# A chunked recurrence on TensorE: token rows of every head in the other half of the partitions, and 64x64 products of channels and tokens alternated with those of a triangular inverse

## The reference, cut to what matters

```python
def step(s, inp):
    r_t, k_t, v_t, kk_t, a_t, w_t = inp
    sa = jnp.einsum("dbhij,dbhj->dbhi", s, kk_t)
    s = (s * w_t[..., None, :] - sa[..., :, None] * (kk_t * a_t)[..., None, :]
         + v_t[..., :, None] * k_t[..., None, :])
    y = jnp.einsum("dbhij,dbhj->dbhi", s, r_t) if readout else None
    return s, y
```

## Time and profile before

| | |
|---|---|
| median of 3 runs | 2006.18 us (2003.2 to 2009.24) |
| the profiled execution's own time | 2008.59 us |
| its span, first to last instruction | 2006.8 us |
| TensorE matmuls busy | 1891.1 us, 94% |
| VectorE, ScalarE, GpSimd busy | 764.0, 476.8, 243.3 us |
| the recurrence, first to last level or y product | from 1193.8 to 1448.3 us |

### The profile page before, as it was taken

One profiled execution on the slowest core, in us unless ns is written; L12 is line 12 of the kernel. 1 busy time (PEld: TensorE's weight loads), 2 busy tenths in 40 slices (PEclk: granted clock), 3 DMA queues, 4 the chain that ended last, 5 costly groups with the idle time before them and its releaser, 6 DMA issues.

```text
span 2006.8 us, 33615 instructions
## 1 busy us (share of the span) xinstructions
PE 1891.1 (94%) x13862; PEld 1003.6 (50%) x13862; DVE 764.0 (38%) x1546; ACT 476.8 (24%) x982; POOL 243.3 (12%) x295
## 2 busy tenths in 40 slices
PE   6999999999999999999899959988898999999997
PEld 2455775444444444434355438888733444444443
DVE  3551441111111100022332347766432888988001
ACT  3022552200000000033211544444322222221001
POOL 1150111000000000012000035465200000000000
PEclk9999799999999999999899979999999999999999
DMA  5421001233432223333311200000021222222222
GB/s 206 168 74 66 30 1 63 97 133 126 147 128 82 84 95 126 105 115 137 118 53 53 69 1 5 5 4 4 15 78 63 74 73 81 75 73 73 84 84 94
DMA packets 43861, 158.63 MB, mean 79 GB/s; under 512 B 5016, under 2 KB 5672, under 8 KB 42712
## 3 DMA queue, kind: packets, MB, share of 16 engines
q1 hardware_dynamic: 37440, 133.19, 19.7%
q10 hardware_dynamic: 6296, 23.58, 3.2%
HBM read 152.01 MB, written 6.31 MB: 79 GB/s over the span
## 4 chain that ended last, share of the span: by engine, by line
PE 88%; DVE 5%; ACT 5%; issue 1%; POOL 1%; DMA 0%; ACTq 0%; DVEq 0%; POOLq 0%
PE psum L330 46%; PE psum L1202 21%; PE psum L1990 2%; PE psum L1994 2%; PE psum L995 2%; PE psum L976 1%; PE psum L589 1%; PE psum L1152 1%; DVE mem L2149 1%; PE psum L963 1%; PE psum L1750 1%; PE psum L632 1%; PE psum L1342 1%; PE psum L2001 1%; DVE mem L2177 1%
## 5 line engine op out<-in xcount | busy, mean ns | idle before, releaser
L330 PE MATMUL psum<-mem 128*128 128x512 f32 (+1 forms) x2272 | 963.0, 582 | 30.3 <-DVE mem L483 15.3
L330 PEld LDWEIGHTS psum<-mem 128*128 128x128 f32 x2272 | 427.4, 190 | 536.4 <-issue 521.3
L1202 PE MATMUL psum<-mem 128*128 128x512 f32 x960 | 421.1, 598 | 4.1 <-DVE mem L2463 2.6
L1202 PEld LDWEIGHTS psum<-mem 128*128 128x128 f32 x960 | 181.7, 191 | 235.7 <-issue 228.0
L2544 DVE SCALAR_TENSOR_TENSOR mem<-mem 128x512 f32<-128x512 f32 x352 | 235.1, 746 | 0.0
L386 POOL TENSOR_TENSOR mem<-mem 128x512 f32<-128x512 f32 x24 | 30.4, 1267 | 1082.4 <-ACT mem L370 1082.0
L1990 PE MATMUL psum<-mem 64*64 64x64 f32 x1920 | 74.5, 222 | 11.7 <-DVE mem L2177 4.4
L1295 ACT ACTIVATE mem<-mem 128x512 f32<-128x512 f32 x22 | 13.9, 630 | 290.7 <-DVE mem L1311 290.7
L1231 DVE SCALAR_TENSOR_TENSOR mem<-psum,mem 128x512 f32 x16 | 12.0, 751 | 179.1 <-PE psum L1202 179.1
L1994 PE MATMUL psum<-mem 64*64 64x64 f32 x1920 | 71.2, 221 | 2.6 <-issue 2.4
L1990 PEld LDWEIGHTS psum<-mem 64*64 64x64 f32 x1920 | 65.0, 136 | 17.3 <-DVE mem L2177 10.0
(11 more groups left out here) (341 smaller groups left out, 1758.8 us busy)
## 6 DMA issues: line engine op xcount, KB each, us to landing
mem<-in_units SPq DMA_DIRECT2D x248, 512.0 KB, 3.4
mem<-in_cw ACTq DMA_DIRECT2D x2, 2048.0 KB, 10.3
mem<-in_wn ACTq DMA_DIRECT2D x1, 2048.0 KB, 8.7
bias_tiles<-bias_scratch ACTq DMA_DIRECT2D x1, 2048.0 KB
mem<-bias_tiles ACTq DMA_DIRECT2D x1, 2048.0 KB, 10.3
mem<-in_xT ACTq DMA_DIRECT2D x1, 2048.0 KB, 9.6
x_scratch<-mem ACTq DMA_DIRECT2D x1, 2048.0 KB, 8.7
mem<-x_scratch ACTq DMA_DIRECT2D x1, 2048.0 KB, 7.8
```

The lines of the kernel that those rows point to most:

```text
L330: last = pe.matmul(dst, ring[:, slot, k, :], rhs(k), start=(k == 0), stop=(k == 7))
L1202: last = eng.matmul(ps[m % 4], ring[:, slot, k - 8 * part, :], rhs(k), start=(k == 0), stop=(k == ktiles - 1))
```

## The change

`FLIP` goes: every head now has its token rows in the half opposite to its channel rows. Levels, fresh, ym and u stay in the straight quarters, and every product between channels and tokens falls into the crossed ones. In TensorE's program seven of the groups are split by direction, and each is issued within a level, one product of the level and one of the group in turn; where a group has a second function, that follows in a run of its own for each `i`. The groups move: x into level 0, raw_beta from after level 4 into level 2, y into level 3, raw_kappa into level 4, state from after level 3 into level 5, turn_v into level 7, turn_bk into level 8. PSUM is laid out anew (level products of a direction share one bank, 0 or 1; the groups have banks 2 to 7), and waits follow it. On VectorE mask_beta stays ahead of grow 5, and move goes from there to ahead of grow 9. Core of the diff:

```diff
-            FLIP = (2, 3)
             E_, O_ = [(0, 0), (1, 0)], [(0, 1), (1, 1)]
             X_ = U_ = Y_ = [(2, 0), (2, 1)]
-            YM_ = [(3, 2), (3, 3)]
-            V_ = S_ = G_ = [(3, 0), (3, 1)]
-            BETA = [(2, 0), (2, 2)]
-            KAPPA = BK = [(3, 0), (3, 2)]
+            S_ = [(2, 2), (2, 3)]
+            YM_ = [(6, 2), (6, 3)]
+            V_ = G_ = [(6, 0), (6, 1)]
+            BETA = [(4, 0), (4, 2)]
+            KAPPA = BK = [(6, 0), (6, 2)]
...
-            def tok(hp, b):
-
-                return ch(1 - b if hp in FLIP else b)
+            def tok(b):
+
+                return ch(1 - b)
...
-                def level(n, d, it):
+                def level(n, d, it, beside=(), done=None):
...
+                    a, b_ = (g[:, :, 1], T) if n % 2 == 0 else (Tt, Z) if n < 9 else (Z, Tt)
+                    at = O_[d] if n % 2 else E_[d]
+                    for i in range(2):
+                        for hp in (i, i + 2):
+                            for b in range(2):
+                                t = tok(b)
+                                own = eng.matmul(dst(at, hp, t), a[t, hp, :], b_[t, hp, :], start=True, stop=True)
+                                for f in beside[:1]:
+                                    other = f(hp, ch(b), t)
+                        for f in beside[1:]:
+                            for hp in (i, i + 2):
+                                for b in range(2):
+                                    other = f(hp, ch(b), tok(b))
+                    own.then_inc(q["made"], 1)
+                    if beside and d:
+                        other.then_inc(both[done], 1)
...
                 for it in range(LAST + 1):
                     for n in range(10):
-                        level(n, 0, it)
-                        level(n, 1, it)
+                        for d in range(2):
+                            if n == 0 and it:
+                                level(n, d, it, x(d, it - 1), "fed")
+                            elif n == 2 and it < LAST:
+                                level(n, d, it, raw_beta(d, it + 1), "beta")
+                            elif n == 3 and lat(it - 1):
+                                level(n, d, it, y(d, it - 1), "y")
+                            elif n == 4:
+                                level(n, d, it, raw_kappa(d, it), "kappa")
+                            elif n == 5 and it:
+                                level(n, d, it, state(d, it - 1), "s")
+                            elif n == 7:
+                                level(n, d, it, turn_v(d, it), "turned")
+                            elif n == 8:
+                                level(n, d, it, turn_bk(d, it), "turned")
+                            else:
+                                level(n, d, it)
...
                 def mask_beta(it):
                     eng.wait_ge(both["beta"], it + 1)
+                    if lat(it - 2):
+                        eng.wait_ge(both["y"], it - 5)
                     mask(BETA, "g1", 0, it, "beta_masked")
...
                     for n in (1, 3, 5, 7, 9):
-                        if n == 5:
+                        if n == 5 and it < LAST:
+                            mask_beta(it + 1)
+                        elif n == 7:
+                            mask_kappa(it)
+                        elif n == 9:
                             if it:
                                 move(it - 1)
                             if it < LAST:
-                                mask_beta(it + 1)
-                        elif n == 7:
-                            mask_kappa(it)
-                        elif n == 9 and it < LAST:
-                            begin(0, it + 1)
-                            begin(1, it + 1)
+                                begin(0, it + 1)
+                                begin(1, it + 1)
```

More of the change, by code:

```diff
@@ L2072, in raw_beta @@
-                def raw_beta(it):
-                    if lat(it - 2):
-                        eng.wait_ge(both["y_kept"], it - 5)
-                    elif it >= 2:
-                        eng.wait_ge(both["u_kept"], it - 1)
-                    raw(BETA, kka, it, "beta")
-                def raw_kappa(it):
-                    if it:
-                        eng.wait_ge(both["moved"], 2 * it + 2)
-                    raw(KAPPA, kd, it, "kappa")
-                def turn_v(it):
-                    eng.wait_ge(both["kappa_masked"], it + 1)
-                    for d in range(2):
-                        n = chunk(d, it)
-                        last = each(lambda hp, c, t: eng.matmul(dst(V_[d], hp, t), vC[c, n, hp, :], ident[c, c], start=True,
-                                                                stop=True))
-                    last.then_inc(both["turned"], 1)
@@ new lines, in raw_beta, with raw_kappa, turn_v @@
+                def raw_beta(d, it):
+                    if it:
+                        eng.wait_ge(both["beta_masked"], it)
+                    return raw(BETA, kka, d, it)
+                def raw_kappa(d, it):
+                    if it:
+                        eng.wait_ge(both["fresh_kept"], it)
+                    if lat(it - 1):
+                        eng.wait_ge(both["ym_kept"], it - 4)
+                    return raw(KAPPA, kd, d, it)
+                def turn_v(d, it):
+                    eng.wait_ge(both["kappa_masked"], it + 1)
+                    n = chunk(d, it)
+                    return [lambda hp, c, t: eng.matmul(dst(V_[d], hp, t), vC[c, n, hp, :], ident[c, c], start=True,
+                                                        stop=True)]
@@ L2112, in pe @@
                             u(it - 1)
-                        elif n == 2 and lat(it - 1):
-                            y(it - 1)
-                        elif n == 3 and it:
-                            state(it - 1)
-                        elif n == 4 and it < LAST:
-                            raw_beta(it + 1)
-                        elif n == 5:
-                            raw_kappa(it)
-                        elif n == 6:
-                            turn_v(it)
-                        elif n == 7:
-                            turn_bk(it)
                         elif n == 9:
                             fresh(it)
-                x(LAST)
+                for d in range(2):
+                    last = each(*x(d, LAST))
+                last.then_inc(both["fed"], 1)
                 ym(LAST)
                 u(LAST)
-                y(LAST)
+                for d in range(2):
+                    last = each(*y(d, LAST))
+                last.then_inc(both["y"], 1)
             def flat(ap):
```

115 lines of the change are left out of this document (50 added, 65 removed).

## The result

The changed kernel takes 2016.61 us (median of 12 runs, 2010.45 to 2021.98), the kernel before 2004.93 (12 runs, 2000.74 to 2010.37). The ratio is 1.0053, with a 95% interval of 1.0037 to 1.0069. Forecast were 1997.0 us and a range of 1985 to 2009: the sign was wrong, and the measured time lies above the range.

A forecast was written before the change was run, and what follows sets the result against it. The prediction took TensorE's instruction blocks, 256 instructions per 3.6 us, as the next bound. Gains of 7.3 us (latent) and 3.5 (context) less 1.5 give 9.3, so 1999.3 profiled, 1997 median; range 1985 to 2009.

The forecast's parts named there:

- the rival at 29 ns a record: Mixed straight and crossed quarters don't run beside each other on TensorE: slower, 2045 to 2062 us; chance 0.05.
- The gates: Waits after T: level 7 for mask_kappa at T + 1.48, level 8 for keep_v at T + 3.40, fresh for keep_bk.
- the 0.69: In levels alternated with two-function groups, the level's last product comes at 0.69 of 0.92 us in its direction.
- The blocks: S to T is 480 records, 3.75 instruction blocks at 3.6 us: 13.5 us, a gain of 1.5 per latent iteration.
- S to T: From the start of level 0 (S) to the end of VectorE's transposes after level 5 (T); 13.5 us forecast, latent.
- The context part: Four context iterations: S to T 10.8 us against 11.56, T to S 7.2 against 7.32; gain 0.9 each, 3.5.
- T to S: From the transposes after level 5 to the next level 0: 7.72 us against 7.44 in a latent iteration, loss 0.3.
- the walk: Hand timing of one latent iteration without block waits: S to T 11.7 to 12.35 us, fresh ending at T + 7.72.
- no change: Rival: blocks take 3.75 to 4.0 us, S to T 14.1 to 15.0, T to S 7.7; 2003 to 2010 us; chance 0.28.
- TensorE's time: Alternated groups in the levels: x and turn_v worth 0.9 us, y, state and turn_bk 0, latent raws 1.55 rather than 1.76.
- more: the blocks don't bind: Rival: the walk holds, a latent iteration takes 19.4 to 20.1 us; 1982 to 1987 us in all; chance 0.12.
- the second one: The rival "no change", which the prediction said would be the forecast by the skill's rule that fetch is hidden.

The follow-up runs named there:

- e9: e1 with a level's eight products alternated with any eight of the group's, the rest of the group last; 1.0026 of the kernel before, 2010.29 us.
- e1: The changed kernel with a group's waits issued for direction 0 alone; 1.0026 of the kernel before, 2007.27 us.
- e7: e4 with 1392 more wait instructions on TensorE, all satisfied, spread over the products; 1.0311 of the kernel before, 2067.48 us.
- e10: e1 with 63 satisfied waits ahead of the first level; 1.0041 of the kernel before, 2011.80 us.
- e4: e2 with the token rows of all heads in the opposite half, groups issued behind their level; 1.0039 of the kernel before, 2009.22 us.
- e2: The change with token rows opposite only in columns 2 and 3, groups behind their levels, waits made once; 0.9974 of the kernel before, 1996.99 us.
- e3: e2 with the groups at the places of the kernel before; 1.0030 of the kernel before, 2006.91 us.
- e11: e3 with move back ahead of grow 5; 1.0004 of the kernel before, 2006.07 us.
- early and late alternation: e4 with x, raw_beta, y, raw_kappa and state alternated with their levels (early, 1.0007), or only turn_v and turn_bk (late, 1.0023).
- e12: e2 with fresh issued behind level 0 of the next iteration; 0.9993 of the kernel before, 2003.38 us.

## Why the prediction was wrong

**What it had right.** Mixed quarters run beside each other: level 0 with x takes 0.46 us a direction, as forecast, and so does level 7 with `turn_v` (1352.03 to 1352.5). The rule of the Trainium skill, "TensorE: Matmul & The Clock Gate", section "Part 3: Packing small matmuls — row/col tiling", that a weight load overlaps running matmuls only if their row groups differ, spoke for the rival at 29 ns a record; this trace, with 14.4, does not agree. The gates are the forecast ones, and in size: level 7 at T + 1.36 (1.48 forecast), level 8 at T + 3.31 (3.40). Grow 5 no longer stands behind `mask_beta`. In level 8 the last own load of direction 0 starts 0.58 after the first (1354.56), ahead of the 0.69, and e9 shows no price of it. The binding resource was named, too: blocks of 256 instructions.

**Step "The blocks": the failed one, by a mis-sized term.** S to T was put at 3.75 blocks of 3.6 us, 13.5. In the iteration shown it measured 14.44, and over the six full latent ones 13.3 to 15.2, on average 14.42. The four blocks from the stand at 1340.22 to the one at 1356.13 took 15.91 us, 3.98 each. The 3.6 came from two pairs of stands; in this trace a block's time isn't constant but moves with the start of its transfer, 1.1 to 2.1 us into the block before. On average that takes 0.92 of the 1.5 us that S to T was to gain. The kernel before averaged 14.80 there, not the 15.06 of the one iteration that was read, so 0.4 was gained. The context part missed by more: forecast were 10.8 for its 3 blocks and 7.2 behind them, 18.0 an iteration, from the shortest of the four before (18.88; on average 12.08 and 7.14). Measured are 12.89 and 8.03. The forecast's stretch from `fresh` to `fresh` would be 230.4 - 7.3 - 3.5 = 219.6 us; it came to 239.6. Of these 20 us the context part has 11.7, and S to T in all ten iterations some 14.

**Step "T to S": a block left out.** It took 7.72 from the walk alone and had no block in it, though 256 records are two blocks (7.2 us at 3.6, less than the walk, but not evenly spread over it). In the changed kernel these records wait for `mask_kappa` and `keep_v` and then come at 14.4 ns, so a block that had been hidden under waits spread out is run through at once and its successor is late: 0.91 us in the middle of level 8. From T the start of `fresh` was to come at 6.80 and comes at 7.65, and the whole is 8.58 us, 0.86 more. Both steps together are 1.8 us in this iteration, one of the slow ones. Over the six full latent iterations T to S is 6.9 to 8.6 us, on average 7.99 (7.45 before), so 0.27 over the forecast, and the two steps together are 22.4 in place of 21.2, and 22.25 before.

**The rival that came nearest** is "no change" (0.28): its mechanism, blocks at 3.75 to 4.0 us, gives S to T 14.1 to 15.0 and T to S 7.7, about what a latent iteration shows. Its time, 2003 to 2010, was passed all the same: by the context part, where it had 11.2 to 12.0 for the measured 12.89, and by the doubled waits, which no rival had.

**Waits counted as free.** I split every group by direction in the walk and left out that each half issues its waits again. e1 prices the second set at some 0.27%, 5 us. Why so much, for instructions that find their semaphore already there, is only partly shown: e7 shows that they fill blocks, and e10 leaves open how far their number alone accounts for it.

**What the opposite rows give up.** The step "TensorE's time" set four quarters in a mixed stream against two in the kernel before, where x and y already ran at 14.4 ns. It called the two-function groups worth 0. So it saw no gain in them, rightly, but it did not price what is lost wherever a group runs alone, except at the end. e4 against e2 shows this price, 0.65%, and the alternation buys back 0.13%, which isn't clear of noise: what it saves in loads (215.8 us busy in e4, 183.4 in e1) comes back as idle time, in S to T as stands.

**`move` ahead of grow 9.** It was called covered, with the remark that "a move that takes 1 us more would show at once". At the old places e3 against e11 gives 0.26%, which the sessions and the profiles don't bear out (see e11). At the new places it was not tried alone, since state comes behind level 5 there. So this stays open.

**The clock** was said to play no part. Of before that is right (1.00 over the stretch). In the changed kernel's profile it costs some 2 us in context iterations. The profile of e1 has 17 us at the lower level behind its first `fresh` and that of e9 none, and both time at 1.0026; but e1's profiled run is its slowest, 2015.17 us against a median of 2007.27, and its three iterations with a fall are 5 us longer than those of e2. So how often the clock falls in the other runs isn't known, and for the medians it isn't shown to be a cause.

**The likeliest reason for the forecast's sign** is that the gain was summed over TensorE's products and the cost over one resource in one half of the iteration. The stage already ran at 3.90 us a block; what made TensorE's loads 10.8 us shorter was handed back as 14.6 us of "issue" and 6.3 us of waits for other engines. Part by part it shows in e1 beside e2: S to T is longer by 9.4 us in all where the products are denser, which is nearly the 10 us between their medians. By the Trainium skill, "Runtime: NRT & Kernel Launch", section "Instruction fetch mechanics", the fetch is hidden. Here its stands are 27.4 us of a 264 us stage, so the measurement decides against it. The rival that follows from that rule is "more: the blocks don't bind", and not the second one, as the prediction has it.

**Still open**: what sets the start of a block's transfer; why early and late alternation don't add; why satisfied waits cost so much; whether `move` has a price; and what made e12 slower.

## What to carry to other kernels

Where TensorE runs many small products, count its instructions, waits included, and divide by the block that the trace shows: a denser packing gains nothing beyond the rate at which the blocks come. Redo the walk of an iteration with the blocks in all of it, also where another wait had hidden them before. And run the parts of a change apart: here the reordering alone (e2) was faster by 0.26%, while opposite token rows, alternation and the waits that came with it took 0.8% away.

## What the runs showed of the hardware that was not expected

- A wait instruction on TensorE whose semaphore is already there isn't free: 1392 of them cost some 55 us of 2013 (1.0311 against 1.0039 of a kernel of 2005 us, e7 and e4), 39 ns each, stands included.
- TensorE stood for up to 1.8 us (2.0 in e1) on an instruction block in the middle of a level, always 256 instructions or a multiple of that, within one, after the stand before.
- No stands at all doesn't mean fast: e4 has none and takes 2009 us, e2 has 16 us of them and takes 1997.
- The granted clock fell to 1.2 GHz in the middle of a stage whose TensorE was busy for 83% of the time (218.74 of 264.26 us), after a stand of 1.6 us and some shorter gaps. It did not fall after two stands of 1.5 us in the same stage, and in e7, with 34 us of stands, it never fell behind the first `fresh`.
